# Long VectorE operations of a two-block kernel done in pieces of 512 to 1024 columns

## The reference, cut to what matters

```python
# each layer: attention over the selected keys, 8 heads
logits = logits + jnp.swapaxes(bias, -1, -2)
logits = jnp.where(valid[:, :, None, :], logits, -jnp.inf)
probs = jax.nn.softmax(logits, axis=-1).astype(c_kv.dtype)
# second block: scan input, skip, and its softmax
xdt = (x * dt[..., None]).reshape(bsz, nc, SSD_CHUNK, ng, hpg, hp)
y = y + d_skip.astype(F32)[:, None] * xs.astype(F32)
pr = jax.nn.softmax(sc, axis=-1).astype(v.dtype)
```

## Time and profile before

| | us |
|---|---|
| median of 3 runs | 1624.06 |
| lowest and highest run | 1622.63, 1637.45 |
| profiled execution, its own time | 1615.94 |
| its span | 1614.1 |
| PE, POOL busy | 1528.9, 1263.8 |
| DVE, ACT busy | 696.7, 714.5 |

### The profile page before, as it was taken

How to read it: one execution, slowest core, us unless ns; L and a number is a source line. 1 busy time by engine, 2 the same in 40 slices (tenths; PEclk the granted TensorE clock), 3 DMA queues, 4 the chain that set the end, 5 groups by cost and what they waited for, 6 DMA issues and landing times.

```text
span 1614.1 us, 21935 instructions
## 1 busy us (share of the span) xinstructions
PE 1528.9 (95%) x7018; PEld 1164.3 (72%) x7018; DVE 696.7 (43%) x1306; ACT 714.5 (44%) x879; POOL 1263.8 (78%) x1509
## 2 busy tenths in 40 slices
PE   7999999999999999989999999999999899999986
PEld 5767877788887777777788887878785656646534
DVE  3995854310126986844301037365454122122225
ACT  4544443544446544534544445546441422315323
POOL 6997897999999996968999999977692533629723
PEclk9999999999999999999999999998999999999998
DMA  6654454677765553444677665645364898999990
GB/s 215 217 172 129 131 156 133 203 212 216 220 207 168 158 157 118 130 136 150 187 220 221 187 206 161 195 131 176 92 208 161 323 345 322 360 364 397 398 365 26
DMA packets 95525, 333.83 MB, mean 207 GB/s; under 512 B 11136, under 2 KB 15760, under 8 KB 94384
## 3 DMA queue, kind: packets, MB, share of 16 engines
q1 hardware_dynamic: 90752, 314.34, 59.0%
q10 hardware_dynamic: 3536, 14.14, 2.6%
q0 software_dynamic: 1152, 4.19, 0.7%
HBM read 322.12 MB, written 21.00 MB: 213 GB/s over the span
## 4 chain that ended last, share of the span: by engine, by line
POOL 54%; PE 25%; issue 14%; DMA 3%; DVE 1%; ACT 1%; POOLq 1%; SPq 0%; DVEq 0%; ACTq 0%
POOL w_lo L1837 53%; PE bank L686 7%; PE bank L1193 5%; PE bank L1247 3%; PE bank L1213 3%; PE bank L1190 2%; PE bank L1263 1%; DMA arena<-in_experts 1%; DMA outputs_by_expert<-xn 1%; PE bank L1303 1%; POOL w_lo L1844 1%; DMA rows_by_expert<-gates,tiny 1%; DMA logits<-outputs_by_expert,tiny 1%; POOLq L1832 0%; PE bank L1088 0%
## 5 line engine op out<-in xcount | busy, mean ns | idle before, releaser
L1837 POOL TENSOR_TENSOR w_lo<-raw,w_hi 128x256 fp32r<-128x256 f32 x1416 | 1069.9, 797 | 132.0 <-ACT w_hi L1417 131.0
L686 PE MATMUL bank<-w_hi,hT 128*128 128x512 f32 x2240 | 714.9, 401 | 37.7 <-POOL w_lo L1837 14.2
L1417 ACT ACTIVATE w_hi<-raw 128x1024 fp32r<-128x1024 f32 x371 | 392.9, 1059 | 530.1 <-PE bank L686 276.4
L686 PEld LDWEIGHTS bank<-w_hi,hT 128*128 128x128 f32 x2240 | 417.1, 191 | 139.9 <-POOL w_lo L1837 21.9
L686 PE MATMUL bank<-w_lo,hT 128*128 128x512 f32 x1120 | 442.3, 395 | 0.0
L1844 POOL TENSOR_TENSOR w_lo<-arena,w_hi 128x1024 fp32r<-128x1024 f32 x61 | 144.6, 2388 | 131.4 <-ACT w_hi L1417 131.2
L686 PEld LDWEIGHTS bank<-w_lo,hT 128*128 128x128 f32 x1120 | 213.5, 191 | 47.0
L997 PE MATMUL bank<-w_hi,mixT 128*128 128x512 f32 x352 | 108.9, 391 | 0.0
L1417 ACT ACTIVATE w_hi<-arena 128x1024 fp32r<-128x1024 f32 x61 | 64.3, 1058 | 77.2 <-DMA arena<-in_experts 28.1
L686 PE MATMUL bank<-w_hi,mixT 128*128 128x512 f32 x288 | 91.6, 399 | 3.8 <-POOL w_lo L1837 2.5
L2248 DVE SCALAR_TENSOR_TENSOR arena<-bank,tiny,arena 128x256 f32<-128x256 f32 x44 | 21.1, 483 | 164.9 <-ACT arena L1573 148.7
(11 more groups left out here) (392 smaller groups left out, 1929.4 us busy)
## 6 DMA issues: line engine op xcount, KB each, us to landing
raw<-in_stream SPq DMA_DIRECT2D x357, 512.0 KB, 3.6
arena<-in_experts SPq DMA_DIRECT2D x154, 512.0 KB, 11.5
raw<-in_experts SPq DMA_DIRECT2D x38, 512.0 KB, 10.7
rows_by_expert<-in_blank ACTq DMA_DIRECT2D x56, 128.0 KB, 3.2
arena<-in_stream SPq DMA_DIRECT2D x9, 512.0 KB, 15.2
gates<-rows_by_expert SPq DMA_DIRECT2D x3, 1024.0 KB, 7.4
outputs_by_expert<-xn SPq DMA_DIRECT2D x3, 1024.0 KB, 5.0
bias_skewed<-bias_windows SPq DMA_DIRECT2D x4, 512.0 KB, 5.2
```

The costliest lines, as they stand in the source:

```text
L686: mm = pe.matmul(LIN[t][:, :], lhs[:, a, k0 + k, t * P:(t + 1) * P], w[:, k, :], start=(k0 + k == 0 and n == 0), stop=(k0 + k == nk - 1 an ...
L1417: act.activation(w_hi[:, s, :], src, ACT.Copy).then_inc(s_hi, 1)
L1837: part = nc.gpsimd.tensor_tensor(w_lo[:, i, c], raw[:, i, c], w_hi[:, i, c].bitcast(F32), ALU.subtract)
```

## The change

Four places issue several operations where they issued one, in the same place of DVE's order. The adding of `keep` is done for two heads at a time, 4 operations of 768 columns for one of 3072. `less_maximum` and `over_sum` share a function that takes four heads at a time of the first part and two heads of the second, so that each operation has 512 columns, six for two. `yb` and `xdt` of the second block are made in 4 operations of 512 columns each. The signals go out with the last operation, as before. That makes 36 more DVE operations: 3 in each of two layers, 4 in each of six softmax places (two in each layer, two in the second block), 6 in group 0. No other engine has an instruction more or less.

```diff
             def less_maximum():
+                i = by_heads(ALU.subtract)
+                i.then_inc(s_arg, 1)
+
+            def by_heads(op):
+
                 for t, v, n in score_parts:
-                    i = dve.tensor_tensor(v, v, row[:, t, :].unsqueeze(2).broadcast_to([P, HEADS_A, n]), ALU.subtract)
-                i.then_inc(s_arg, 1)
+                    k = 4 - 2 * t
+                    for h in range(0, HEADS_A, k):
+                        i = dve.tensor_tensor(v[:, h:h + k], v[:, h:h + k],
+                                              row[:, t, h:h + k].unsqueeze(2).broadcast_to([P, k, n]), op)
+                return i
 
             def over_sum():
                 own(dve.reciprocal(tiny[:, 208:224], tiny[:, 208:224]))
-                for t, v, n in score_parts:
-                    i = dve.tensor_tensor(v, v, row[:, t, :].unsqueeze(2).broadcast_to([P, HEADS_A, n]), ALU.mult)
+                i = by_heads(ALU.mult)
                 i.then_inc(s_nx, 1)
...
-                own(dve.tensor_tensor(logits[:], bias[:], keep.unsqueeze(1).broadcast_to([P, HEADS_A, WIN]), ALU.add))
+                for h in range(0, HEADS_A, 2):
+                    i = dve.tensor_tensor(logits[:, h:h + 2], bias[:, h:h + 2],
+                                          keep.unsqueeze(1).broadcast_to([P, 2, WIN]), ALU.add)
+                own(i)
...
-                        skip = small[:, S_DS:S_DS + 16].unsqueeze(1).broadcast_to([P, TT, 16])
-                        dve.tensor_tensor(by_head(yb), by_head(xs), over(skip), ALU.mult)
-                        dve.tensor_tensor(by_head(xdt), by_head(xs), over(dt), ALU.mult).then_inc(s_nx, 1)
+                        skip = small[:, S_DS:S_DS + 16]
+                        for t in range(TT):
+                            for c in (0, 8):
+                                dve.tensor_tensor(by_head(yb)[:, t, c:c + 8], by_head(xs)[:, t, c:c + 8],
+                                                  skip[:, c:c + 8].unsqueeze(2).broadcast_to([P, 8, 64]), ALU.mult)
+                        for t in range(TT):
+                            for c in (0, 8):
+                                i = dve.tensor_tensor(by_head(xdt)[:, t, c:c + 8], by_head(xs)[:, t, c:c + 8],
+                                                      dt[:, t, c:c + 8].unsqueeze(2).broadcast_to([P, 8, 64]), ALU.mult)
+                        i.then_inc(s_nx, 1)
```

## The result

The changed kernel takes 1634.43 us (median of 20 runs), the kernel before beside it 1625.95 us (20 runs). The ratio is 1.0044 with a 95% interval of 1.003 to 1.0058: **7.2 us slower** (4.9 to 9.4), within the 1% that was called no change. The forecast was 1631 us, +7.5. As the experiments show, the sum is better than its terms.

What follows compares the result with a forecast made beforehand. In the front part PE and POOL run at nearly the same pace and whichever is behind sets it. Terms -0.6 + 2.2 + 1.2 - 1.3 + 4.5 + 1.5 = +7.5 on 1624.06 gave 1631 us, range 1614 to 1643.

Steps and rivals of the forecast that it cites:

- Turns, one and one: Wherever POOL is busy: every DVE operation costs DVE its own columns and one POOL subtraction, 1.14 us per 512 columns.
- No turns between pieces: Rival, chance 0.12: DVE keeps the port over operations close together, POOL stands as long as before; -1 to +3 us, 1625.
- L2324: Adding of keep in pieces, two layers: POOL saves 0.3 us each time, -0.6 us; DVE's later end is hidden by idle time.
- First layer: less_maximum and over_sum in pieces make DVE late and PE wait for it: +2.2 us, and +1.2 for the clock.
- the clock term: First layer: after PE's stop of 3.5 us the granted clock may fall; loss 0 to 2.8 us, +1.2 taken.
- Nothing returns it: First layer: the +2.2 us stays lost, since until 300 us POOL waits 9.3 us for slots PE hasn't freed.
- Second layer: The earlier hold of L2227 (6.28 us) doesn't come, so it takes the changed first layer's time: -1.3 us; held again, +3.4.
- Second block: Group 0: DVE's pieces end 5.4 us later and PE waits for its read, +4.5 us, plus +1.5 for the clock.
- The branch written for that case: Second block: if POOL gets no turn during L2725 and L2728, only less_maximum grows, and it is +1.8 us.
- the main branch: Second block: POOL gets turns between pieces from 1077.9 us on, DVE pays for them; +4.5 us and +1.5 for the clock.
- POOL's time counts: Rival, chance 0.27: PE's waits for POOL shrink and DVE's delay doesn't matter; -7.8 us, 1616 us.
- More holds: Rival, chance 0.08: added operations bring three new holds on PE's path, 4.6 us each above the sum; 1645 us.

Runs made afterwards that it cites:

- the port kernel: Two kernels, computing nothing of the reference, that set two-operand DVE operations beside POOL subtractions: trains every 0.86, 1.13, 1.67 and 2.73 us, no hold in single arrivals.
- the layers alone: Changed kernel with only less_maximum and over_sum of the two layers in pieces of 512 columns, other places whole: 1.0033 against the kernel before, +5.4 us.
- the pause: Changed kernel with a 1-column memset and a wait for it behind each of the four xdt pieces: 1.008 against the kernel before, +13.0 us.

## Why the prediction held, and where its steps were off

1. **Turns, one and one: right** where both engines have work queued. 6.68 us for a place (6.6 forecast), 1.18 us for L1837 beside it, and the cadences of the port kernel. "No turns between pieces" is out in the layers. It was right for xdt and prob, where the prediction had it as a branch.
2. **L2324:** -0.6 forecast, PE's wait went from 1.25 to 1.02 us in the first layer: -0.2 there, nothing seen in the second.
3. **First layer:** the two waits for DVE came as said (3.28 us at 208.18, forecast 208.8; 3.71 at L921, whose start was forecast at 228.9 and came at 230.31). The delay was 6.6 us in this profile in place of 3.4. The mechanism was right and the clock term mis-sized: +1.2 was taken, 0 to 2.8 allowed; with the same stops it was 0 in the layers alone and 4.0 here, since there are two stops and the clock can fall after both. "Nothing returns it" was right (the delay changes by 0.1 us from 250 to 300), but its reason is read one step short: the earlier trace rows has POOL waiting for ACT's `w_hi`, and the same view has ACT waiting 23.8 us for PE and 14.8 for DMA.
4. **Second layer:** no hold, as forecast, but +2.3 and not -1.3. The clock fell after both waits here too (0.57 from 685 to 693 us, 0.66 from 709 to 714); in the layers alone it fell once and the layer cost +0.5.
5. **Second block:** +4.5 and +1.5 forecast, +2.4 measured. The step that failed is "In pieces I expect turns from 1077.9 on": POOL was held for 4.77 us, as it was in every profile with these pieces and no pause, and as the earlier trace rows had shown it between L2725 and L2728. The branch written for that case said +1.8. With the pause, which brings the turns, the stretch costs 5.7: the price of the main branch (6.0) was right, its condition not met.
6. **The baseline:** the sum was made against an execution that is 10 us better than its median, and that median was taken for chance. Part of it has a name: a hold in the first layer (3.5 us, in the three other profiles with less_maximum whole and the branch reads unedited) and one of 9.6 us at next_gain (over 7 us, in three profiles). The change removes the first and pays its turns with it. So the first layer of before is probably some 3.5 us dearer in a typical execution than the forecast had it, and the pieces' 2.6 to 6.6 stand against that. In the profiles the changed places cost 6.6 + 2.3 + 2.4 = 11.3 us where the forecast had 7.5; between the medians it was 7.2. That errors of this size cancelled, and the sum came out to 0.3 us, is luck; that DVE's lateness makes the kernel slower by some us isn't.
7. **POOL's time counts (1616 us): wrong.** POOL's busy time is the same to 0.3 us. In the first layer PE's waits for POOL (1.23, 1.67 and 1.09 us) are gone, and 3.28 and 3.71 us for DVE stand in their place. "More holds": the added operations had one, on POOL's side, which had been there before (4.39 us).

Not settled: what makes a hold. Nor is the profile's delay outside the changed places (16.3 less 6.6, 2.3 and 2.4, that is 5.0) traced to its last part.

## What to carry to other kernels

Where two engines take turns at a port, cutting an operation doesn't give the other engine time: it adds one of the other's operations to each piece, as long as the other has one queued. So ask who waits for the engine whose work is cut, and put the reads that a busy engine waits for between the pieces. And compare a profile with its own median first: if it is 10 us better, look for what the typical execution has and this one hasn't, before its rows are summed.

## What the runs showed of the hardware

- With both engines queued, DVE operations with two SBUF operands and POOL's subtractions go one and one: a DVE operation comes every 0.86, 1.13, 1.67 and 2.73 us for 256, 512, 1024 and 2048 columns beside a subtraction of 256, which is some 0.59 us for the turn and 1.05 ns a column. The Trainium skill (SBUF — State Buffer, "Who interferes with whom") says that issue order decides who blocks; the runs add that the turns alternate. Beside an idle POOL six pieces of 512 columns took 3.70 us, beside a busy one 6.68.
- They don't always. DVE was held behind 9 subtractions (6.3 us) and 14 (9.65, an operation of 8 columns); POOL behind seven DVE operations (4.77). The holds of 6.3 and 9.6 us ended with POOL's row, those of 4.77 with DVE's row of two-operand operations. None of 176 arrivals in the kernels of the port alone gave one, so the moment against the other engine doesn't explain them in the steps tried; the condition is open. In one profile, in both layers, a held place that was edited away handed the hold to the next two-operand operation (7.41 and 4.67 us); at next_gain it didn't.
- The same stops of PE (3.3 and 3.7 us) were followed by a granted clock of 0.50 in one execution and 1.00 in another (of another version of the kernel), a difference of 4.0 us in one layer.
